# Triangular inverse from blocks of 4, decay formed in both orientations, decay rows loaded a head ahead, a semaphore per merged block, and a plain last store, in a one-core hybrid decoder layer

## The chip, the cores and the metric

One Trainium2 chip, one of its cores. The metric is the device time of one execution in microseconds. TensorE is called PE, VectorE DVE, ScalarE ACT, GpSimd POOL and SyncE SP, as in the profile's rows.

## The reference

One decoder layer on x of 512 tokens by 2048 channels, float32. h is the RMS-normed x. One projection of h gives the q, k, v, z of eight delta-rule heads (branch A, 128 wide), beta and alpha of each, the q, k, v, z of eight block-sparse attention heads (branch B), and two gates of 2048 channels. Branch A is what the change is about:

```python
cum_g = jnp.cumsum(g, axis=-1)
decay_mat = jnp.exp(jnp.where(causal, cum_g[..., :, None] - cum_g[..., None, :], -jnp.inf))
kk = jnp.einsum("nbhid,nbhjd->nbhij", k, k)
a_mat = jnp.where(strict, beta[..., :, None] * kk * decay_mat, 0.0)
sol = lax.linalg.triangular_solve(eye + a_mat, rhs, left_side=True, lower=True, unit_diagonal=True)
...
merged = jax.nn.sigmoid(g_gdn) * y_gdn + jax.nn.sigmoid(g_moba) * y_moba
x = x + jnp.einsum("btd,de->bte", merged, w_o[l])
```

The kernel uses chunks of 128 tokens in place of 64, four to a head, and forms the inverse of I + A instead of solving. Both branches then go through an up-projection to 2048 channels, are gated, added, and projected by w_o; x is added.

## The kernel before, in words

**Exact products.** Every large product of float32 matrices is three PE products of rounded parts: high by high, high by low, low by high. ACT makes the high part (`split` in the scalar block), DVE the low one.

**Head loop (0 to 977 us).** For each of eight heads, eight stripes of 128 columns of w_in are projected: `win(w, a, b)` issues the k-steps a to b of stripe w, 16 in all, each of three matmuls of 512 columns (lines 740 to 744). Between these pieces PE executes the small fp32 steps of the head: transposes and products of 128 x 128, one for each of four chunks (`four`, `turn`). The order on every engine is written out by hand in its `head(h, p)`; p is the head before, whose attention is finished in the first two stripes of the next head. Heads 1 to 6 are a hardware loop on DVE, ACT and POOL, heads 1 to 7 on PE; head 0 and the last one are written apart.

**The inverse.** L is minus the strict lower part of beta k k' decay. `cgrow` makes decayT = exp(row - column + mask); POOL masks it (`dTs`); DVE multiplies it with k k' (`kk`, into Up), PE transposes Up (`UT`), DVE multiplies the result by -beta (Ln), PE transposes that again (`LT`), and DVE cuts blocks of 16 out of both. `n1` to `n4` form (I + L)(I + L^2)(I + L^4)(I + L^8) for the blocks of 16. `ma` and `mb`, three times, merge two blocks each: to 32, to 64, to 128. `ma` multiplies the part of L below the diagonal blocks (`lm[1]`, `lm[2]`, masked by POOL) by the inverse so far and transposes the inverse; ACT and DVE copy the two results (Yt, XTt); `mb` multiplies them; DVE adds. The last merge works on corners of 64 x 64.

**Decay rows.** `cg_dram` holds the cumulated decay of each head as a row; POOL loads it, copied to all partitions, at the head's start (`decay_row`).

**Last head.** Ten steps `own_step` (2048 columns each, on DVE) put sums of parts of h into `own`, and POOL stores four stages of it (`store_own`); a step that overwrites the tile waits for the store before it.

**Products by quads (978 to 1642 us).** Gates (4 quads), up-projections (2 for each branch) and w_o (2 quads) are computed as 2 x 2 blocks with seven products instead of eight (P11, P12, PS1, PS2, PS4, PS3, P22). A unit is 1024 columns of weights; ACT rounds them (`op_hi`), DVE takes the rest (`op_lo`), four units ahead of PE. DVE's `block_add` finishes a block. In the quads YB and YB + 1 (branch B) DVE multiplies the block by its gate, and POOL adds branch A's block by an accumulating DMA (`finish_block`), one after the other, under the one semaphore `part_added`; PE then transposes the merged block (`merged_turn`). The quads from W0 on are stored by accumulating DMAs into `out`, where x has been copied before.

## Time and profile before

| | us |
|---|---|
| median of 3 runs (1638.84 to 1641.06) | 1639.57 |
| the profiled execution, its time | 1643.32 |
| its span, first to last instruction | 1641.8 |
| PE busy | 1592.5 (97%) |
| DVE busy | 1092.7 (67%) |
| ACT busy | 790.1 (48%) |
| POOL busy | 158.3 (10%) |
| mean granted PE clock | 0.994 |

A row of a timeline gives start and duration, engine, line and operation, output <- inputs, and in brackets how long the engine was idle before it and what released it. PE's rows overlap: a matmul's duration has its way through the array in it, so the cost of a group is read from the starts of what follows. PEld are weight loads. A plain fp32 matmul shows as two records (x8 is four matmuls), a transpose as one. DVE's durations overlap by some 0.08 us as well.

### The profile page before, as it was taken

The numbers are of one execution on the slowest core, as the hardware profiler recorded it, in microseconds if no ns is written. First come the engines' busy times: TensorE is split into PE (matmuls) and PEld (weight loads), VectorE is DVE, ScalarE is ACT, GpSimd is POOL, SyncE is SP. The second block draws the span as 40 slices with busy tenths as digits, with TensorE's granted clock in tenths as the row PEclk, the third lists the DMA queues.
The fourth block names the chain that finished last, engine by engine and source line by source line (L and its number), as shares of the span: only waits on it lengthen the run. The fifth ranks groups of instructions, "written<-read, shape, count | busy, mean of one in ns | idle before, by whom it ended". The sixth has DMA issues, their size and how long they took to land.

```text
span 1641.8 us, 20823 instructions
## 1 busy us (share of the span) xinstructions
PE 1592.5 (97%) x7858; PEld 1316.3 (80%) x7858; DVE 1092.7 (67%) x1320; ACT 790.1 (48%) x1048; POOL 158.3 (10%) x154
## 2 busy tenths in 40 slices
PE   6999999999999999999999999999999999999997
PEld 5888888887887887887887887888888778777885
DVE  5745745645646646556568758867677999888863
ACT  5434534435434444335335346556465845447442
POOL 4101001001001000010011011011010000001011
PEclk9999999999999999999999999999999999999999
DMA  8304314223223233133143337576566556775653
GB/s 261 78 26 115 84 38 129 57 76 90 77 57 99 73 77 96 51 89 83 51 113 101 137 136 210 192 192 220 140 189 187 196 196 209 202 217 112 196 116 52
DMA packets 192379, 206.19 MB, mean 126 GB/s; under 512 B 7491, under 2 KB 139846, under 8 KB 190726
## 3 DMA queue, kind: packets, MB, share of 16 engines
q1 hardware_dynamic: 176470, 161.69, 33.2%
q0 software_dynamic: 15856, 43.80, 11.2%
q8 instruction: 33, 0.54, 0.1%
q14 instruction: 20, 0.16, 0.0%
HBM read 180.28 MB, written 29.38 MB: 128 GB/s over the span
## 4 chain that ended last, share of the span: by engine, by line
PE 81%; issue 6%; DVE 5%; DMA 5%; ACT 2%; POOL 1%; SPq 0%; ACTq 0%; POOLq 0%; DVEq 0%
PE bank L740 14%; PE bank L744 14%; PE bank L742 14%; PE bank L1161 8%; PE bank L1163 8%; PE bank L1165 8%; PE bank L769 6%; DMA e_block<-branch_a 2%; PE bank L774 1%; DVE ring_lo L2117 1%; PE bank L930 1%; PE bank L946 1%; DMA operands<-branch_a 1%; ACT ring_hi L1520 1%; PE bank L940 1%
## 5 line engine op out<-in xcount | busy, mean ns | idle before, releaser
L740 PE MATMUL bank<-h_hi_r,w_hi 128*128 128x512 f32 x1008 | 421.5, 418 | 0.0
L744 PE MATMUL bank<-h_hi_r,w_raw_r 128*128 128x512 f32 x1008 | 396.9, 394 | 0.0
L742 PE MATMUL bank<-h_lo_r,w_hi 128*128 128x512 f32 x1008 | 394.1, 391 | 0.0
L2117 DVE TENSOR_TENSOR ring_lo<-operands,ring_hi 128x1024 fp32r<-128x1024 f32 x224 | 271.8, 1221 | 117.8 <-ACT ring_hi L1520 116.8
L1520 ACT ACTIVATE ring_hi<-operands 128x1024 fp32r<-128x1024 f32 x224 | 235.5, 1059 | 230.0 <-PE bank L1165 174.4
L744 PEld LDWEIGHTS bank<-h_hi_r,w_raw_r 128*128 128x128 f32 x1008 | 189.1, 188 | 43.0
L742 PEld LDWEIGHTS bank<-h_lo_r,w_hi 128*128 128x128 f32 x1008 | 190.3, 189 | 35.6 <-issue 1.7
L740 PEld LDWEIGHTS bank<-h_hi_r,w_hi 128*128 128x128 f32 x1008 | 189.9, 188 | 35.8 <-issue 1.7
L1161 PE MATMUL bank<-ring_hi,h_hi_r 128*128 128x512 f32 x480 | 190.6, 397 | 3.1 <-issue 3.1
L1163 PE MATMUL bank<-ring_lo,h_hi_r 128*128 128x512 f32 x480 | 189.4, 395 | 0.0
L1674 DVE TENSOR_TENSOR w_raw_r<-w_raw,w_hi 128x2048 fp32r<-128x2048 f32 x64 | 146.7, 2292 | 45.9 <-ACT w_hi L1219 44.7
L1165 PE MATMUL bank<-ring_hi,h_lo_r 128*128 128x512 f32 x416 | 162.4, 390 | 0.0
L1165 PE MATMUL bank<-ring_hi,sums_r 128*128 128x512 f32 x384 | 150.1, 391 | 0.0
L1161 PE MATMUL bank<-ring_hi,sums_r 128*128 128x512 f32 x320 | 126.3, 395 | 7.6 <-DVE ring_lo L2117 4.3
L1163 PE MATMUL bank<-ring_lo,sums_r 128*128 128x512 f32 x320 | 125.1, 391 | 0.0
L1219 ACT ACTIVATE w_hi<-w_raw 128x2048 fp32r<-128x2048 f32 x64 | 122.2, 1909 | 0.0
L1161 PEld LDWEIGHTS bank<-ring_hi,h_hi_r 128*128 128x128 f32 x480 | 90.4, 188 | 24.5 <-issue 4.1
L1163 PEld LDWEIGHTS bank<-ring_lo,h_hi_r 128*128 128x128 f32 x480 | 90.7, 189 | 18.5 <-issue 0.2
L1165 PEld LDWEIGHTS bank<-ring_hi,h_lo_r 128*128 128x128 f32 x416 | 78.4, 188 | 17.3
L1165 PEld LDWEIGHTS bank<-ring_hi,sums_r 128*128 128x128 f32 x384 | 72.5, 189 | 15.6
L1161 PEld LDWEIGHTS bank<-ring_hi,sums_r 128*128 128x128 f32 x320 | 60.4, 189 | 22.5 <-issue 7.2
L1163 PEld LDWEIGHTS bank<-ring_lo,sums_r 128*128 128x128 f32 x320 | 60.5, 189 | 12.3
(324 smaller groups left out, 2179.4 us busy)
## 6 DMA issues: line engine op xcount, KB each, us to landing
w_raw<-in_w_in_dram SPq DMA_DIRECT2D x64, 1024.0 KB, 6.0
operands<-in_w_in_dram SPq DMA_DIRECT2D x64, 512.0 KB, 4.7
operands<-in_w_o_dram SPq DMA_DIRECT2D x32, 512.0 KB, 4.9
operands<-in_w_in_dram POOLq DMA_DIRECT2D x16, 512.0 KB, 8.7
gates<-e_block POOLq DMA_DIRECT2D x16, 512.0 KB, 5.3
operands<-in_w_out_gdn_dram SPq DMA_DIRECT2D x16, 512.0 KB, 4.0
operands<-gates SPq DMA_DIRECT2D x16, 512.0 KB, 5.2
operands<-in_w_out_moba_dram SPq DMA_DIRECT2D x16, 512.0 KB, 4.6
```

The lines of the kernel that those rows point to most:

```text
L740: pe.matmul(PJ[slot % 2][:], w_hi[slot % 2][:, c], h_hi[:, k, :], start=(k == 0), stop=False, skip_group_check=True)
L742: pe.matmul(PJ[slot % 2][:], w_hi[slot % 2][:, c], h_lo[:, k, :], start=False, stop=False, skip_group_check=True)
L744: mm = pe.matmul(PJ[slot % 2][:], w_lo[slot][:, c], h_hi[:, k, :], start=False, stop=(k == KT - 1), skip_group_check=True)
L769: mm = pe.matmul(ps[:, tile4(t)], lhsT[:, tile4(t)], rhs[:, tile4(t)], start=True, stop=True)
L774: mm = pe.transpose(ps[:, tile4(t)], src[:, tile4(t)], ident[:])
L1161: pe.matmul(ps[:], a_hi, ring_hi[:, n % RINGS, c], start=(FRESH[p] and k == 0), stop=False, skip_group_check=True)
L1163: pe.matmul(ps[:], a_hi, ring_lo[:, n % RINGS, c], start=False, stop=False, skip_group_check=True)
L1165: mm = pe.matmul(ps[:], a_lo, ring_hi[:, n % RINGS, c], start=False, stop=(k == kn - 1), skip_group_check=True)
L1219: act.activation(w_hi[slot % 2][:], raw[slot][:], ACT.Copy).then_inc(s["hi_ready"], 1)
L1520: act.activation(ring_hi[:, n % RINGS, :], operand(q, p, j), ACT.Copy).then_inc(s["op_hi"], 1)
L1674: dve.tensor_tensor(w_lo[slot][:], raw[slot][:], w_hi[slot % 2][:].bitcast(F32), ALU.subtract)\
L2117: dve.tensor_tensor(ring_lo[:, n % RINGS, :], operand(q, p, j), ring_hi[:, n % RINGS, :].bitcast(F32), ALU.subtract).then_inc(s["op_lo"], 1)
```

## The change

- The inverse starts from blocks of 4: (I + L)(I + L^2), two small products instead of four steps, then five merges (to 8, 16, 32, 64, 128; `LEVELS`). A merge at level b of the first four moves only the 64 columns that belong to the lower halves of its pairs, and uses only the first 128 - b rows and columns; DVE masks the product while it copies it (`paired`), so L need not be masked ahead; ACT copies the transpose.
- The decay is formed in both orientations: `cgrow` makes dT and dL; POOL multiplies dL by -beta and by the mask of the blocks of 4, dT by that mask and by a row of -beta. DVE multiplies k k' by dTb and dLm (Ud, Ld), and by dL (Ln). The two transposes UT and LT are gone. `cg_dram` and `rows2` hold two rows a head, loaded while the head before runs. Head 0 gets its second row by four more matmuls, and one more transpose. `cgrow` stands ahead of `split(n + 1)` on DVE and ahead of `evac(p, 7)` on ACT.
- The masks are made at the start by nine DVE passes from the identity, which is loaded first.
- `own_step` 8 to 10 are cut into halves and stand at other places.
- `acc[i]`, one semaphore for each block, replaces `part_added`. For W0, POOL's `add_22` waits for the transpose of the block of the same number. In quads YB and YB + 1, `block_add` stands ahead of `op_lo`.
- The last block: x is loaded and added by DVE before PE is done, tile 0 is added when PE has finished it (`tile_done`), and SP stores both tiles plainly.

```diff
@@ sync @@
+            sp.dma_start(ident[:], consts[:, C_ID, :]).then_inc(s["ident_loaded"], 16)
             load_x(0)
             sp.dma_start(nw[:], norm_w.broadcast_to([P, D])).then_inc(s["nw_loaded"], 16)
-            sp.dma_start(ident[:], consts[:, C_ID, :]).then_inc(s["ident_loaded"], 16)
...
+            sp.dma_start(residual, token_block(xs, LAST, 3)).then_inc(s["stage_b"], 16)
+            for t in range(2):
+                sp.wait_ge(s["c_add"], 2 * (4 * LAST + 3) + 1 + t)
...
+                sp.dma_start(token_block(outs, LAST, 3)[:, t, :], block(LAST, 3)[:, t, :]).then_inc(s["stage_b"], 16)
+            sp.wait_ge(s["stage_b"], 16 * 5)
@@ gpsimd @@
+            def decay_parts(h):
+
+                pool.wait_ge(s["cg_dl"], h + 1)
+                pool.tensor_tensor(q4(dL), q4(dL), hcb(HC_NB), ALU.mult).then_inc(s["cg_dts"], 1)
...
+                pool.tensor_tensor(q4(dTb), q4(dT), over(masked4[:]), ALU.mult).then_inc(s["cg_dts"], 1)
...
+                pool.tensor_tensor(q4(dLm), q4(dL), over(masked4[:]), ALU.mult).then_inc(s["cg_dts"], 1)
...
+                pool.tensor_tensor(dTb[:], dTb[:], nb_row, ALU.mult).then_inc(s["cg_dts"], 1)
...
-                pool.wait_ge(s["cg_dt"], h + 1)
-                pool.wait_ge(s["n3_mm"], h)
-                pool.tensor_tensor(q4(dTs), q4(dT), over(plane(C_STRICT)), ALU.mult).then_inc(s["cg_dts"], 1)
+                decay_parts(h)
+                if p is None:
+                    store_rows()
+                if h is not last:
+                    decay_row(h + 1)
...
-                    if b > 0:
-                        pool.wait_ge(s["part_added"], 16 * b)
-                    pool.dma_start(e, m_dram[q - YB, k], accum_op=ALU.add).then_inc(s["part_added"], 16)
+                    pool.dma_start(e, m_dram[q - YB, k], accum_op=ALU.add).then_inc(acc[i], 16)
@@ tensor @@
             def n1(h):
...
-                four(G0, Ud, Ld)
-                four(G1, Ld, Ud).then_inc(s["n1_mm"], 1)
+                four(G0, Ud, Ld).then_inc(s["n1_mm"], 1)
...
             def ma(h, k):
...
+                    m = P - b
+                    for t in range(NT):
+                        pe.matmul(G0[:m, t * PAIRED:(t + 1) * PAIRED], Ln[:, t * P:t * P + m],
+                                  half_tile(xa, t, b, 1), start=True, stop=True)
+                    for t in range(NT):
+                        mm = pe.transpose(G1[:m, t * P:t * P + m], xa[:m, t * P:t * P + m], ident[:m, :m])
...
             def mb(h, k):
...
+                    m = P - LEVELS[k]
+                    for t in range(NT):
+                        mm = pe.matmul(G2[:m, t * PAIRED:(t + 1) * PAIRED], XTt[:m, t * P:t * P + m],
+                                       Yt[:m, t * PAIRED:(t + 1) * PAIRED], start=True, stop=True)
...
-                UT(h)
+                n1(h)
                 win(2, 12, 14)
                 ss(h, 1)
-                win(2, 14, 15)
-                LT(h)
-                win(2, 15, 16)
-                win(3, 0, 1)
+                win(2, 14, 16)
+                n2(h)
+                win(3, 0, 2)
                 qk(h)
...
+                win(4, 10, 12)
                 vTs(h)
...
+                win(4, 12, 13)
+                pe.wait_ge(s["X"], NL * h + NL - 1)
+                pe.wait_ge(s["vb"], h + 1)
                 win(4, 13, 14)
-                ma(h, 2)
+                ma(h, 4)
@@ vector @@
             def kk(h):
                 dve.wait_ge(s["kk_mm"], h + 1)
-                dve.wait_ge(s["cg_dts"], h + 1)
...
-                dve.tensor_tensor(Up[:], G2[:], dTs[:], ALU.mult).then_inc(s["kkd"], 1)
+                dve.wait_ge(s["cg_dts"], 4 * h + 4)
...
+                dve.tensor_tensor(Ud[:], G2[:], dTb[:], ALU.mult).then_inc(s["Ud"], 1)
...
+                dve.tensor_tensor(Ld[:], G2[:], dLm[:], ALU.mult).then_inc(s["Ld"], 1)
...
+                    dve.tensor_tensor(y, g, pairs, ALU.mult).then_inc(s["Y"], 1)
...
+                    b, m = LEVELS[k], P - LEVELS[k]
+                    x = half_of(xa, b, 1)[:m]
+                    g = compact(G2, m).rearrange("p (n b) -> p n b", b=b)
+                dve.tensor_tensor(x, g, x, ALU.add).then_inc(s["X"], 1)
```

The order of the instructions, at three places. First PE in the head loop, from the first step behind `kk` to the transposes of v. The rows of projection between them are left out; `work` and `inv` are the tiles of the powers and of the inverse. Before:

```order
L774 MATMUL bank<-ident,lower 128x128 x4
...
L769 MATMUL bank<-work 128x128 x8
...
L769 MATMUL bank<-work 128x128 x8
L769 MATMUL bank<-inv_a,work 128x128 x4
...
L769 MATMUL bank<-inv_b,lower 128x128 x4
L774 MATMUL bank<-ident,inv_b 128x128 x4
```

Now:

```order
L818 MATMUL bank<-inv_a,work 128x128 x4
...
L894 MATMUL bank<-inv_a,lower 124x64 x4
L897 MATMUL bank<-ident,inv_a 124x124 x4
...
L912 MATMUL bank<-work 124x64 x4
...
L894 MATMUL bank<-inv_a,lower 120x64 x4
L897 MATMUL bank<-ident,inv_a 120x120 x4
```

The long groups of full products are gone; between the pieces of projection there are now smaller groups, two for each merge.

Second DVE in the loop, between `n2` and the merge of blocks of 8 (`pairs` is the mask). Now:

```order
L1813 TENSOR_TENSOR work<-bank,pairs 124x256
...
L1709 TENSOR_TENSOR w_raw_r<-w_raw,w_hi 128x2048
L1828 TENSOR_TENSOR inv_a<-bank,inv_a 124x64x4
...
L1813 TENSOR_TENSOR work<-bank,pairs 120x256
...
L1741 TENSOR_SCALAR conv_gv<-raw_gv,chan 128x512
```

The split of a weight stripe stands between Y(0) and X(0), and the convolution of v between Y(1) and X(1).

Third DVE at the end of the program, behind PE's last units. Before:

```order
L2130 TENSOR_TENSOR e_block<-e_block,bank 128x512 x2
L2117 TENSOR_TENSOR ring_lo<-operands,ring_hi 128x1024 x4
L2132 TENSOR_TENSOR e_block<-bank,e_block 128x512 x4
```

Now:

```order
L2187 TENSOR_TENSOR e_block<-e_block,bank 128x512 x2
L2167 TENSOR_TENSOR ring_lo<-operands,ring_hi 128x1024 x4
L2189 TENSOR_TENSOR e_block<-bank,e_block 128x512 x2
L2373 TENSOR_TENSOR e_block<-e_block,operands 128x1024
L2189 TENSOR_TENSOR e_block<-bank,e_block 128x512 x2
```

The pass that adds x stands between the third block and the last one.

## Rows read from the trace of the kernel before

**Rows 1.** Busy time by stretch: us, PE, PEld, DVE, ACT, POOL, clock, DMA share, GB/s

```profile
153.08:270.81 117.73, 117.73 (x616) 97.77 (x615) 65.97 (x99) 50.88 (x77) 9.37 (x8) 1.00 0.29 79
```

**Rows 2.** Timeline of PE in head 1, projection rows left out

```profile
188.15 0.60 PE L774 MATMUL bank<-ident,work 128*128 128x128 f32 x4
...
213.27 1.05 PE L769 MATMUL bank<-inv_b,lower 128*128 128x128 f32 x8
214.16 0.60 PE L774 MATMUL bank<-ident,inv_b 128*128 128x128 f32 x4
...
216.68 1.06 PE L769 MATMUL bank<-work 128*128 128x128 f32 x8
...
219.66 1.05 PE L769 MATMUL bank<-inv_a,lower 128*128 128x128 f32 x8
...
226.14 0.67 PE L863 MATMUL bank<-inv_b,lower 64*64 64x64 f32 x8
226.75 0.41 PE L866 MATMUL bank<-ident,inv_b 64*64 64x64 f32 x4
```

**Rows 3.** Timeline of PE's weight loads in head 0

```profile
51.32 0.30 PEld L1075 LDWEIGHTS bank<-mgt,ones_f 128*128 128x128 f32 x2
51.55 0.19 PEld L740 LDWEIGHTS bank<-h_hi_r,w_hi 128*128 128x128 f32 x1
```

**Rows 4.** Timeline of DVE in head 1, and its first pass of head 2

```profile
186.65 0.68 DVE L1738 TENSOR_TENSOR work<-bank,work 128x512 f32<-128x512 f32 x1
...
199.18 2.55 DVE L1709 SCALAR_TENSOR_TENSOR conv_gv<-raw_gv,chan,conv_gv 128x512 f32<-128x512 f32 x3
...
212.09 0.69 DVE L1784 TENSOR_TENSOR v_beta<-bank,hcol 128x512 f32<-128x512 f32 x1 [1.85 <-PE bank L774]
...
270.81 2.29 DVE L1674 TENSOR_TENSOR w_raw_r<-w_raw,w_hi 128x2048 fp32r<-128x2048 f32 x1 [6.20 <-ACT w_hi L1219]
```

**Rows 5.** Timelines of POOL and DVE in the last head

```profile
895.89 3.28 POOL L654 TENSOR_TENSOR lower<-lower,cst 128x512 f32<-128x512 f32 x1 [13.11 <-DVE lower L1743]
...
898.44 1.28 DVE L1727 TENSOR_TENSOR conv_gq<-conv_gq,raw_gq 128x512 f32<-128x512 f32 x1 [0.44 <-ACT raw_gq L1286]
```

**Rows 6.** Timelines of ACT, DVE, POOL and PE in head 0

```profile
60.79 0.63 ACT L1261 ACTIVATE decayT<-decayT 128x512 f32<-128x512 f32 x1
...
60.66 4.09 DVE L1709 SCALAR_TENSOR_TENSOR conv_gq<-raw_gq,chan,conv_gq 128x512 f32<-128x512 f32 x3
...
62.89 1.30 POOL L644 TENSOR_TENSOR work<-decayT,cst 128x512 f32<-128x512 f32 x1
...
65.86 0.66 PE L774 MATMUL bank<-ident,conv_gk 128*128 128x128 f32 x4 [0.25 <-DVE conv_gk L1727]
```

**Rows 7.** Timeline of POOL in the last head, and DMA issues: count, size, median us

```profile
916.67 0.53 POOL L673 DMA_DIRECT2D row_sums<-sg  x1 [15.29 <-DVE sg L2077]
...
row_sums<-sg POOLq DMA_DIRECT2D x4, 1024.0 KB, 6.1
```

**Rows 8.** PE's waits (total, times, longest), and PE and ACT behind the merged blocks

```profile
PE bank L1177 <- DMA e_block<-branch_a: 5.7, 5, 1.9
...
1484.58 0.76 PE L1161 MATMUL bank<-ring_hi,sums_r 128*128 128x512 f32 x1 [3.29 <-issue]
...
1478.16 1.92 ACT L1607 ACTIVATE sums_r<-h_hi 128x2048 fp32r<-128x2048 f32 x1 [3.67 <-DVE h_hi L2077]
```

**Rows 9.** PE alone by stretch, behind an idle time of 3.12 us: us, busy, clock, DMA

```profile
1340.00:1345.00 5.00, 5.00 (x16) 0.66 1.02 373
```

**Rows 10.** DVE and POOL at the end, and DMA issues: count, size, median us

```profile
1629.91 1.29 DVE L2132 TENSOR_TENSOR e_block<-bank,e_block 128x512 f32<-128x512 f32 x2 [7.47 <-PE bank L1165]
...
1631.50 1.20 POOL L714 DMA_DIRECT2D out_dram<-e_block  x1 [7.56 <-DVE e_block L2132]
...
out_dram<-e_block POOLq DMA_DIRECT2D x8, 512.0 KB, 7.1
branch_outputs<-work POOLq DMA_DIRECT2D x8, 256.0 KB, 2.3
```

More of the change, by code:

```diff
@@ L53 @@
 NQ = W0 + W_QUADS
+LAST = NQ - 1
 BLOCK_ROW, BLOCK_COL = (0, 0, 1, 1), (0, 1, 1, 0)
@@ L101, in added @@
 def added(q):
-    return 16 * (sum(ku(b) == 4 for b in range(q)) + 1)
+    return 16 * (sum(ku(b) == 4 or b >= YB for b in range(q)) + 1)
 def op_loads(q, j, slot, nth=0):
@@ L278, in hybrid_layer @@
         w0_ = sb("work0", [P, T], at=area)
-        lm = [sb(f"lower{i}", [P, T], at=area) for i in range(3)]
+        Ln, dL, dLm = [sb(f"lower{i}", [P, T], at=area) for i in range(3)]
         xa = sb("inv_a", [P, T], at=area)
@@ L782, in cgrow @@
                                    start=True, stop=True)
+                for t in range(NT):
+                    mm = pe.matmul(G1[:, tile4(t)], hcol[:, HC_NB, t:t + 1].broadcast_to([P, P]), ident[:],
+                                   start=True, stop=True)
                 mm.then_inc(s["cgrow_mm"], 1)
@@ L856, in ma @@
-                if k < 2:
-                    pe.wait_ge((s["L32m"], s["L64m"])[k], h + 1)
-                    four(G0, lm[k + 1], src)
-                    mm = turn(G1, src)
+                    pe.wait_ge(s["X2"], h + 1)
+                    pe.wait_ge(s["qkd"], h + 1)
+                elif k < NL - 1:
+                    pe.wait_ge(s["X"], NL * h + k)
+                if k == NL - 1:
+                    for t in range(NT):
+                        i, j = tile4h(t)
+                        pe.matmul(G0[:P // 2, j], Ln[P // 2:, i], xa[P // 2:, j], start=True, stop=True)
+                    for t in range(NT):
+                        i, j = tile4h(t)
+                        mm = pe.transpose(G1[:P // 2, i], xa[:P // 2, i], ident[:P // 2, :P // 2])
@@ L1687, in cgrow @@
                     dve.wait_ge(s["cg_rows"], 16 * (NT + h))
-                row = G2 if first else cgb
+                row = G2 if first else cg_row
                 dve.wait_ge(s["hcol"], h + 1)
-                dve.wait_ge(s["cg_dts"], h)
-                for t in range(NT):
-                    dve.scalar_tensor_tensor(dT[:, tile4(t)], row[:, tile4(t)], hcol[:, HC_CG, t:t + 1],
-                                             plane(C_DMASK), ALU.subtract, ALU.add).then_inc(s["cg_arg"], 1)
+                dve.tensor_tensor(q4(dL), q4(row), hcb(HC_CG), ALU.subtract).then_inc(s["cg_arg"], 1)
+                dve.wait_ge(s["cg_arg"], 3 * h + 1)
+                dve.tensor_tensor(q4(dT), q4(dL), over(plane(C_DMASK)), ALU.add).then_inc(s["cg_arg"], 1)
+                dve.tensor_tensor(q4(dL), q4(dL), over(plane(C_CMASK)), ALU.subtract).then_inc(s["cg_arg"], 1)
             def conv(h, c):
@@ L2124, in block_add @@
                 e, p = block(q, i), BLOCK_PRODUCT[i]
-                dve.wait_ge(s["pe_unit"], ended(q, p))
+                tiles_apart = q == LAST and i == 3
+                if not tiles_apart:
+                    dve.wait_ge(s["pe_unit"], ended(q, p))
                 dve.wait_ge(s["e_copy"], 8 * q + (2, 6, 8, 8)[i])
@@ L2288, in _ @@
                 q, p, j = place(n)
+                for qb in range(NQ):
+                    for i in range(4):
+                        if YB <= qb < W0 and n == ended(qb, BLOCK_PRODUCT[i]) + LEAD - 1:
+                            block_add(qb, i)
                 op_lo(n)
@@ L2291, in _ @@
                     for i in range(4):
-                        if n == ended(qb, BLOCK_PRODUCT[i]) + LEAD - 1:
+                        if not YB <= qb < W0 and n == ended(qb, BLOCK_PRODUCT[i]) + LEAD - 1:
                             block_add(qb, i)
```

405 lines of the change are left out of this document (207 added, 198 removed).

## The prediction, before the changed kernel was run

> **What bounds the kernel now.** I read the busy time by stretch first. One pass of the head loop takes 117.7 us and TensorE (PE) is busy for all of it [rows 1]; so in seven of the eight heads only what PE executes, or a wait that does not exist yet, can move the time. Then the PE timeline inside one head, for the price of each record [rows 2, 3]; then VectorE (DVE) and ScalarE beside it, for the room each hand-over has [rows 4]; last PE's waits outside the loop [rows 6 to 8] and what follows PE's last matmul [rows 10].
>
> **Prices on PE.** A plain fp32 matmul is two records, a transpose one, a projection matmul (512 columns) one. In [rows 2] the first inverse step runs 8 records from 213.27 to 214.16: 0.111 us each. From 213.27 to 216.68 stand 8 records, 4 transposes and 9 projection matmuls (3.41 us); from 216.68 to 219.66 8 records and 9 projection matmuls (2.98). So 4 transposes cost 0.43 (0.108 each) and a projection matmul 0.23. The 64-column corner takes 0.61 for 8 records, 0.076 each.
>
> **1. The inverse on PE.** Removed per head: 40 full matmuls (4 of the first squaring's 8, 8 of the 12 behind it, the 12 of n3 and n4, the 16 of the first two merges) and 16 transposes (UT, LT and two merges): 80 + 16 = 96 records, at 0.111 10.7 us. Added: 32 matmuls that move 64 columns (64 records) and 16 transposes, all with 124, 120, 112 or 96 weight columns. No row has 124 x 64. Below, the 64 x 64 price, 0.076. Above, 0.111: two weight loads whose matmuls move only 32 columns still stand 0.115 apart [rows 3], so fewer moving columns alone bring nothing; the load seems to set the pace. I take a price that falls with the weight columns, between 0.076 at 64 and 0.111 at 128: 0.109, 0.107, 0.102, 0.094, mean 0.103. 80 records: 8.2 us. **Saved: 2.4 us a head, 19.4 in eight** (14.2 if all cost 0.111; 33 if the 64 half-width records cost 0.076).
> The Trainium skill (TensorE: Matmul & The Clock Gate, section LDWEIGHTS) gives the load as weight columns / 1.2 ns, which is 94 ns as a mean of the four widths; by it, with the 0.004 by which the measured 0.111 stands above its 107 ns, the sum would be 2.8 us a head. The 0.115 rows agree with its value for 128 columns.
>
> **2. Room of each hand-over in a steady head.** Ten steps of the merge take turns with three k-steps of projection (9 matmuls, 2.1 us). Counting in my prices from n2 as zero: qk 2.3, ma0 5.2, mb0 8.6, ma1 11.5, mb1 14.9, ma2 17.9, mb2 21.3, ma3 24.2, mb3 27.6, transposes of v 29.9.
> - n1 now needs two products (Ud, Ld) at kk instead of one. The one of before starts at 186.65; two at a spacing of 0.60 end at 187.95, and the step in that slot starts on PE at 188.15 [rows 2, 4]: covered by 0.2 us.
> - The split of 2.3 us between Y(0) and X(0): 7.1 to 9.4, PE's mb0 ends 9.7. Covered.
> - The convolution of v, 3.6 us (three taps are 2.55 [rows 4], with the first tap and the clamp), lies between Y(1) and X(1): 13.4 to 17.1, X(1) at 17.5, ma2 due at 17.9. Covered by 0.4, the tightest.
> - SiLU of v: ScalarE's three passes end at 22.4, X(2) at 23.3, ma3 due at 24.2. Covered by 0.9.
> - ma4 now waits for vb in the same window: the transposes last 0.60 [rows 2], DVE 0.69 more [rows 4] with 0.04 between, so vb stands 1.33 after their start; PE arrives after 0.43 + 3 x 0.23 = 1.12. **New wait 0.2 us a head, 1.8 in all** (0 to 6: the 0.4 and 0.2 above may not hold).
> - The decay: three 512-wide DVE passes instead of four small ones, one more exponential, four POOL passes instead of three. DVE sits idle for 6.2 us at the head's start [rows 4] and rows are loaded a head ahead, so the passes fall in there; POOL's four end some 25 us before kk. Nothing in heads 1 to 7. Without that idle time DVE would owe 2 us.
>
> **3. Head 0 has no such room.** PE: 4 more matmuls for the second row (0.89) and one transpose: +1.0. Then POOL's four passes (1.3 each alone [rows 6]) start when the second exponential is done. The first ran from 60.79 [rows 6]; PE's row is 0.9 later and ScalarE has a copy and an exponential more, so POOL starts at some 62.7. There DVE is about to begin the taps of q, 2 us later than the 60.66 of before (0.9 from PE, 0.8 from its own three wider passes, 0.3 for a second copy). A POOL pass and a DVE pass with two SBUF inputs shut each other out: POOL's pass stretches from 1.30 to 3.28, DVE's norm from 0.69 to 1.28 [rows 4 to 6], and three taps took 4.09 beside one POOL pass and its DMAs, 2.55 without [rows 4, 6]. Alternating, the taps end near 67.9, POOL near 69, the norm of k at 69.6, and PE, ready at 66.6 (65.86 less its wait of 0.25 [rows 6], plus 1.0), waits 3.0 instead of 0.25. n1 then waits 1.3 where its slot waited some 0.3 (kk stands behind a split of 2.3). Together some +3.4. A wait of this length is the sort after which the clock fell: after 3.1 us idle, the next 5 us ran at a mean of 0.66 [rows 9], 1.7 us lost; I put in half, 0.8. **Head 0: +5.2** (1 to 9).
>
> **4. Last head.** own_step 8 moves to 3.6 us after own_step 7; before there were 9. It overwrites what a POOL DMA of 1 MB still reads, issued as soon as step 7 ends and landing after 6.1 (median) [rows 7]. DVE then waits 2.7 us, with split(n+5) and Y(3) queued behind it, and PE's mb3 has 1.3 of room less the 1.2 us half-step: **+2.5** (0 to 6).
>
> **5. Merged blocks.** PE waits 5.7 us in five places for the adding DMAs [rows 8], each of which waited for the one before. With a semaphore each they go out when the product is gated, and block_add no longer queues behind op_lo (1.1 us earlier); landing 7 us later is in time. I call 4.1 of it the first quad's (three waits of 0.9 to 1.9) and book that. The second quad's share I give back: behind it PE waits 3.29 at 1484.58 for the first row sum, whose rounding on ScalarE had waited 3.67 for DVE's step [rows 8]; DVE's queue, not the DMA, sets that, so the wait grows to 5. **-4.1** (2 to 6).
>
> **6. Last store.** Now DVE adds from 1629.91 to 1631.20 behind PE, then the adding DMA leaves at 1631.50 and the span ends at 1641.8 [rows 10]. New: tile 0 is added while PE works, tile 1 ends at 1630.6, and a plain 256 KB store leaves. Plain 256 KB stores land in 2.3 us, adding ones of 512 KB in 7.1 [rows 10]; between 2.3 and 5, with issue and the closing waits, I take the end at 1634.8: **-7** (5 to 8.5). Block 2's adding DMA, issued 8.7 us earlier than the last, would land about then too.
>
> Constants first (ident before x) and the nine mask passes of DVE: the second x tile, which the start waits for, is issued third or fourth as before; 0 (-0.3 to +0.6).
>
> **Sum:** -19.4 + 1.8 + 5.2 + 2.5 - 4.1 - 7 = -21.0 us. The profiled execution took 1643.3 (span 1641.8), the median of the runs is 1639.6; with the same difference: **1619 us**.
>
> **Rivals.**
> - **A, width counts, not weights:** half-width records at 0.076. 64 x 0.027 x 8 = 14 more: 1605. For it: the corner's 0.076; against: the 0.115 of [rows 3]. 0.13.
> - **B, the steps get tight:** X(1) or Ld comes late and each head pays about 1 us: 1627. For: 0.2 and 0.4 us of room; against: the engines' chains are fixed ones of known length and nothing else stands in those queues. 0.14.
> - **C, the end stays:** the third block's adding DMA or POOL's closing wait ends last, so the last store brings 2, not 7: 1624. 0.10.
> - **D, slower, pieces:** the merges read and write pieces of 4, 8, 16 or 32 words with gaps, where all is contiguous before. If a record that moves such pieces takes more than twice its 0.1 us, or a DVE pass over them more than its room, PE gains nothing. At 0.21 a record instead of 0.103, the 32 piecewise records a head cost 3.4 us more: +27, 1646. It decides from 0.19 a record on. No row shows pieces so short; against it, the corner's tiles (64 in 128) run at 0.076. 0.05.
> - The forecast keeps 0.58.
>
> **Range and chances.** Worst sum of likely ends (records at 0.111, head 0 +8, last head +5, tail -5) gives 1632; the best (half the way to A, head 0 +2, last head 0) 1606. The range **1606 to 1632** leaves out D and the far half of A. A measurement here can tell about 0.2%, 3.3 us, from no change: slower by that needs D, 0.05; within it, B and all bad ends together, 0.04; faster 0.91.
>
> **What would show it.** Steady heads: period 115.5 us (117.7 before), 113.8 if A holds; a wait of some 0.2 us before the 64-column corner and nothing else over 0.3. The 124 x 64 group of 12 records in 1.3 us. In head 0 a wait of about 3 us before the transposes of k with DVE's taps stretched beside POOL; in the last head one before mb3. At the merges no DMA wait in the first quad, but a longer one at the row-sum product behind the second. The end 5 us after PE's last matmul. Wrong it would be if the periods were not below 117, or if waits of 1 us stood in every head.

## The result, and the profile after

The changed kernel took **1625.3 us** (median of 4 runs, 1624.4 to 1626.5), the kernel before beside it 1640.3 (1638.8 to 1641.9): ratio 0.991, 95% interval [0.989, 0.992], 15.0 us less. The forecast was 1619 in a range of 1606 to 1632. The direction and the range held, but the sum of 21 us was made of terms of which only some were right, and their errors partly cancelled.

A steady head, by stretch, from the transposes of k in head 1 to those in head 2 (columns as in [rows 1]):

```profile
185.79:300.67 114.88, 114.71 (x599) 94.96 (x598) 65.26 (x99) 50.77 (x76) 12.16 (x9) 1.00 0.31 83
```

Before it was 117.73 [rows 1]: 2.85 us less. TensorE is still busy for all but 0.17 us. Its rows in head 3, projection rows left out, answer to [rows 2]:

```profile
428.37 0.98 PE L894 MATMUL bank<-inv_a,lower 128*124 128x64 f32 x8
429.18 0.59 PE L897 MATMUL bank<-ident,inv_a 124*124 124x124 f32 x4
...
434.62 0.95 PE L894 MATMUL bank<-inv_a,lower 128*120 128x64 f32 x8
435.41 0.58 PE L897 MATMUL bank<-ident,inv_a 120*120 120x120 f32 x4
...
440.79 0.91 PE L894 MATMUL bank<-inv_a,lower 128*112 128x64 f32 x8
441.53 0.55 PE L897 MATMUL bank<-ident,inv_a 112*112 112x112 f32 x4
...
446.86 0.81 PE L894 MATMUL bank<-inv_a,lower 128*96 128x64 f32 x8
447.51 0.50 PE L897 MATMUL bank<-ident,inv_a 96*96 96x96 f32 x4
```

Read from start to start, the eight records of ma take 0.81, 0.79, 0.74 and 0.65 us: 0.101, 0.099, 0.093 and 0.081 each as a mean over the group, where I had put 0.109 to 0.094 and a full record of before takes 0.111 [rows 2]. What a record costs inside the group stands under experiments 4 and 5.

Head 0, DVE's timeline (the taps of q, the clamp, the norm of k), answer to [rows 6]:

```profile
62.61 4.92 DVE L1744 SCALAR_TENSOR_TENSOR conv_gq<-raw_gq,chan,conv_gq 128x512 f32<-128x512 f32 x3
67.56 1.37 DVE L1747 TENSOR_SCALAR raw_gq<-conv_gq 128x512 f32<-128x512 f32 x1
68.85 0.68 DVE L1762 TENSOR_TENSOR conv_gk<-conv_gk,raw_gk 128x512 f32<-128x512 f32 x1
```

POOL's timeline beside it:

```profile
62.54 1.04 POOL L683 TENSOR_TENSOR lower<-lower,hcol 128x512 f32<-128x512 f32 x1 [22.07 <-ACT lower L1304]
63.54 1.75 POOL L687 TENSOR_TENSOR work<-decayT,masked 128x512 f32<-128x512 f32 x1
65.25 1.73 POOL L690 TENSOR_TENSOR lower<-lower,masked 128x512 f32<-128x512 f32 x1
66.94 1.71 POOL L694 TENSOR_TENSOR work<-work,decay_rows 128x512 f32<-128x512 f32 x1
```

PE's waits outside the steady heads, from its timeline (in brackets the wait and what ended it):

```profile
69.58 0.66 PE L823 MATMUL bank<-ident,conv_gk 128*128 128x128 f32 x4 [2.99 <-DVE conv_gk L1762]
74.23 1.13 PE L818 MATMUL bank<-work 128*128 128x128 f32 x8 [1.02 <-DVE work L1773]
...
853.34 0.46 PE L976 MATMUL bank<-ident,bv 128*128 128x128 f32 x1 [3.82 <-DVE bv L1913]
...
919.53 1.54 PE L912 MATMUL bank<-work 96*96 96x64 f32 x8 [4.14 <-DVE work L1813]
...
1474.60 0.77 PE L1198 MATMUL bank<-ring_hi,sums_r 128*128 128x512 f32 x1 [8.27 <-issue]
```

Head 0 waits as forecast (3.0 and 1.3). At 919.53 stands the wait of the last head that was forecast (2.5), at 853.34 one that was not. No transpose of a merged block waits 0.25 us or more for its DMA, and the row-sum product behind the second quad waits 8.27 instead of 3.29 [rows 8].

The first of the two on DVE's timeline of the last head (its last row belongs to the second wait):

```profile
837.49 2.35 DVE L2142 TENSOR_TENSOR sg<-h_hi_r 128x1024 f32<-128x1024 f32 x2
839.88 2.36 DVE L2142 TENSOR_TENSOR sg<-sg,h_lo_r 128x1024 f32<-128x1024 f32 x2
842.15 0.68 DVE L1725 TENSOR_TENSOR lower<-decay_rows,hcol 128x512 f32<-128x512 f32 x1
...
847.16 3.47 DVE L1709 TENSOR_TENSOR w_raw_r<-w_raw,w_hi 128x2048 fp32r<-128x2048 f32 x1 [2.99 <-ACT w_hi L1258]
...
915.71 1.23 DVE L2142 TENSOR_TENSOR sg<-h_hi_r 128x1024 f32<-128x1024 f32 x1 [4.38 <-DMA row_sums<-sg]
```

POOL beside it:

```profile
848.44 3.31 POOL L694 TENSOR_TENSOR work<-work,decay_rows 128x512 f32<-128x512 f32 x1
```

DVE at the same place of head 6:

```profile
722.72 0.69 DVE L1725 TENSOR_TENSOR lower<-decay_rows,hcol 128x512 f32<-128x512 f32 x1
...
728.85 2.37 DVE L1709 TENSOR_TENSOR w_raw_r<-w_raw,w_hi 128x2048 fp32r<-128x2048 f32 x1 [4.11 <-ACT w_hi L1258]
```

own_step 1 and 2 (4.7 us) stand ahead of the decay passes. These passes now stand ahead of the split of the next stripe, and their exponentials ahead of ScalarE's rounding that the split waits for. The passes are 4.5 us later than in head 6 (842.15 less 114.88 is 727.3), the split 3.4, and it stretches from 2.4 to 3.5 beside POOL's fourth pass. The clock behind the two waits (by stretch; PEclk is the third number from the end):

```profile
853.00:858.00 5.00, 4.66 (x13) 3.47 (x14) 3.75 (x9) 2.28 (x7) 0.00 (x0) 0.66 0.00 0
919.00:924.00 5.00, 4.47 (x17) 3.79 (x18) 3.49 (x6) 1.89 (x3) 0.00 (x0) 0.50 0.00 0
```

The tail, answer to [rows 10]: first DVE's two tiles, then SP's two plain stores. PE's last matmul starts at 1619.55.

```profile
1618.70 0.69 DVE L2189 TENSOR_TENSOR e_block<-bank,e_block 128x512 f32<-128x512 f32 x1 [5.06 <-PE bank L1202]
1619.97 0.69 DVE L2189 TENSOR_TENSOR e_block<-bank,e_block 128x512 f32<-128x512 f32 x1 [0.58 <-PE bank L1202]
```

The stores, from the DMA issues (count, size, median us to landing):

```profile
out_dram<-e_block SPq DMA_DIRECT2D x2, 256.0 KB, 2.2
```

The span ends at 1623.3, 3.8 us after PE's last start; before it was 12.3 (1629.5 to 1641.8).

**The ledger.** I take landmarks on PE: the transposes of k in head 0 (65.86 before, 69.58 now), the corner's mb of each head, the product of the second row sum, the last matmul.

| stretch | forecast | measured |
|---|---|---|
| eight heads, 2.82 a head with the new wait in it | -17.6 | -22.6 |
| head 0 beside that | +5.2 | +4.1 |
| last head beside that (corner to corner 127.2 now, 118.3 before) | +2.5 | +11.8 |
| merged blocks to the row sum | -4.1 | see below |
| end | -7 | -8.5 |

Without the fourth line that is -15.2, and the medians say -15.0. The two profiled spans say -18.5 (1641.8 to 1623.3). The difference is the fourth line. The profiled execution of before lay 3.0 us above its kernel's median (1643.3 against 1640.3), that of the changed kernel 0.45 below.

### The profile page after: what moved, and what is told of

It reads as the page before. It is cut to its first block, busy times and chain, and to the rows that moved or that the text cites. A ratio compares the mean times of both kernels' runs of the same rounds, so it can differ in the third digit from the quotient of the medians.

```text
span 1623.3 us, 20700 instructions
## 1 busy us (share of the span) xinstructions
PE 1572.4 (97%) x7739; PEld 1297.6 (80%) x7739; DVE 1091.4 (67%) x1333; ACT 788.8 (49%) x1049; POOL 176.4 (11%) x161
## 4 chain that ended last, share of the span: by engine, by line
PE 83%; DVE 10%; issue 3%; DMA 2%; ACT 2%; SPq 0%; POOL 0%; DVEq 0%; ACTq 0%
PE bank L789 14%; PE bank L793 13%; PE bank L791 13%; PE bank L1198 10%; PE bank L1200 10%; PE bank L1202 10%; DVE ring_lo L2167 2%; PE bank L818 2%; PE bank L912 1%; PE bank L894 1%; PE bank L966 1%; PE bank L982 1%; DVE w_raw_r L1709 1%; PE bank L897 1%; PE bank L823 1%
```

## Experiments

Each ran beside the kernel before, whose median in the four sessions was 1641.0, 1641.8, 1640.4 and 1640.8. "The changed kernel" is 1625.3 throughout, from a session of its own; since the same kernel moved by 1.5 us between sessions, a difference of that size from it shows nothing by itself.

### 1. The decay rows ahead of the own steps (e1_rows_first)

```diff
                     columns(h)
+                    cgrow(h)
                     if h is last:
                         own_step(1)
                         own_step(2)
-                    cgrow(h)
                     split(n + 1, 1)
```

> In the last head the changed kernel's PE waits 3.82 us at 853.34 for softmax's bv and runs at a granted 0.66 behind it (head period 120.6 instead of 114.9, so 5.7 us). Here own_step 1 and 2 stand behind cgrow instead of ahead of it, nothing else moves. Theory 'queue': the 4.7 us of own steps held back the decay rows, and with them ScalarE's two exponentials and the rounding that the split waits for; the split was due at 843.7 and own steps now end at some 844.2: wait under 0.5 us, about 5.5 us gained, 1620. Rival 'shared port': POOL's four decay passes (4.9 us alone) now run beside the four own halves, which read two SBUF tiles each; they shut each other out, own steps end at 848 to 849 instead of 844, the split starts there, and PE's wait is 4 to 6 us again: 1625 to 1627.

Measured 1627.1 (1626.0 to 1627.4), ratio 0.991 [0.990, 0.993]: no gain. DVE's timeline in the last head:

```profile
839.31 3.20 DVE L2142 TENSOR_TENSOR sg<-h_hi_r 128x1024 f32<-128x1024 f32 x2
842.54 4.44 DVE L2142 TENSOR_TENSOR sg<-sg,h_lo_r 128x1024 f32<-128x1024 f32 x2
846.91 3.38 DVE L1709 TENSOR_TENSOR w_raw_r<-w_raw,w_hi 128x2048 fp32r<-128x2048 f32 x1
```

POOL's:

```profile
841.39 2.27 POOL L687 TENSOR_TENSOR work<-decayT,masked 128x512 f32<-128x512 f32 x1
843.63 2.27 POOL L690 TENSOR_TENSOR lower<-lower,masked 128x512 f32<-128x512 f32 x1
845.86 2.28 POOL L694 TENSOR_TENSOR work<-work,decay_rows 128x512 f32<-128x512 f32 x1
```

The rows come at their place, but the four own halves take 7.6 us instead of 4.7 and POOL's passes 2.3 instead of 1.3. The split ends where it ended in the changed kernel (850.3 and 850.6), and PE waits 3.44. The theory "queue" fell and the rival "shared port" held: whichever of the two stands first, 4.7 us of own steps and 4.9 us of POOL passes do not fit ahead of the split. The Trainium skill (SBUF — State Buffer, section SBUF: two separate sides) calls the port pair of the two engines an exclusive lock held for a whole instruction. The trace comes close to that: a POOL pass follows the next after 2.24 us here, where one takes 1.27 alone and a DVE half pass 1.17, 2.44 together.

### 2. The own steps moved away from both places (e2_spread)

Step 1 stands where 3 stood, 2 where 4 stood, 3 where 5 stood; 4 and 5 behind mb0 and mb1, 6 behind mb3, 7 behind mb4. POOL's stores of them follow: the first stands with the second and third, the last behind its other stores. And:

```diff
                 kS(h, 3)
+                if h is last:
+                    own_step(8)
+                    own_step(9)
                 o_lo_(h)
...
                 bvTs(h)
+                if h is last:
+                    own_step(10)
```

> All ten own steps of the last head move later, into idle places of DVE behind the decay rows (1 in the slot of 3, 2 in that of 4, 3 in that of 5, 4 and 5 behind mb0 and mb1, 6 behind mb3, 7 behind mb4, 8 and 9 behind the last kS, 10 behind bvTs), and POOL's stores follow them. If both waits of the last head (3.82 at 853.34, 4.14 at 919.53, each with a clock of 0.5 to 0.66 behind it) are made by where the own steps stand, both vanish, the last head's period becomes 114.9 to 115.5 and the gain over the changed kernel is 11 to 12.5 us: 1613 to 1614. If the rows' new exponentials and POOL's four passes are what makes the last head late by themselves, the first wait stays (gain 6). If the sums come too late for the first sum product (998 in the changed kernel), a wait appears there instead, 1616 to 1620.

Measured **1614.0** (1613.4 to 1614.1), ratio 0.984 [0.982, 0.985]. Both waits are gone, and from head 6 to the last head it takes what a steady head takes (by stretch, from the transposes of k to those of the last head):

```profile
760.20:875.08 114.88, 114.71 (x599) 94.97 (x598) 70.24 (x103) 50.74 (x76) 11.60 (x8) 1.00 0.29 78
```

So the last head's 11.8 us are the placing of ten passes, of which the change moved only the last three, and the decay's new passes by themselves cost that head nothing.

### 3. Only the step that waited for its store, and those behind it (e10_own8)

```diff
-                if h is last:
-                    own_step(8, 0)
                 split(n + 5, 1)
                 ma(h, 3)
                 zclamp(h, 0)
-                if h is last:
-                    own_step(8, 1)
                 mb(h, 3)
+                if h is last:
+                    own_step(8, 0)
                 vTs(h)
+                if h is last:
+                    own_step(8, 1)
...
```

Steps 9 and 10 and POOL's last store move back with it, to the places that the expectation gives.

> The changed kernel with own_step 8 behind mb3 (halves around the transposes of v), 9 behind mb4 and split(n + 6), 10 behind the last kS, POOL's last store behind its others: own steps 1 to 7 stay. Theory: step 8 then starts some 10 us after the store of step 7 was issued, so DVE does not wait for it; PE's wait of 4.14 before mb3 and the slow clock behind it go, 5.5 to 6.1 us, and the first wait of 3.8 stays: 1619 to 1620. Rival 'the waits hide each other': the second wait moves to another place of the last head, 1623 to 1625.

Measured 1619.7 (1618.1 to 1621.0), ratio 0.987 [0.986, 0.989]. The wait at 919.53 is gone, that of 3.81 at 853.68 stays. So 5.7 us belong to the store that step 8 waited for, and the 5.7 that experiment 2 gained beyond it belong to the start of the head.

### 4 and 5. What sets the price of a small record (e3_w128, e4_mov128)

All 128 weight columns with 64 moved, and then the other way round:

```diff
-                        pe.matmul(G0[:m, t * PAIRED:(t + 1) * PAIRED], Ln[:, t * P:t * P + m],
+                        pe.matmul(G0[:, t * PAIRED:(t + 1) * PAIRED], Ln[:, t * P:(t + 1) * P],
                                   half_tile(xa, t, b, 1), start=True, stop=True)
```

> ma's first product loads all 128 weight columns in the four piecewise merges instead of 124, 120, 112 and 96; it still moves 64. Theory 'weights set the pace': its 8 records take 0.89 us instead of 0.81, 0.79, 0.74 and 0.65, 0.57 us a head more, steady period 115.45 instead of 114.9, total +4.5 us, 1630. Rival 'the rows moved or the output's rows set it, and 0.08 to 0.11 is only the spread of small matmuls': no change, 1625.3.

```diff
-                        pe.matmul(G0[:m, t * PAIRED:(t + 1) * PAIRED], Ln[:, t * P:t * P + m],
-                                  half_tile(xa, t, b, 1), start=True, stop=True)
+                        pe.matmul(G0[:m, t * P:(t + 1) * P], Ln[:, t * P:t * P + m],
+                                  xa[:, t * P:(t + 1) * P], start=True, stop=True)
```

> The same product with the weights of the change (124 to 96 columns) but all 128 columns of the inverse moved instead of 64; DVE reads the needed half out of the product in pieces. Theory 'weights set the pace': 8 records stay at 0.81, 0.79, 0.74, 0.65 or rise little, steady period within 0.1 us of 114.9, 1625 to 1626. Rival 'moving columns set the pace' (rival A of the prediction): up to 0.89 each, +0.5 us a head or more, 1630. DVE's piecewise read of the product costs at most some tenths beside PE; if it makes a wait, it shows before mb.

Measured 1627.9 (1625.2 to 1630.5) and 1628.6 (1626.8 to 1629.7), ratios 0.993 [0.991, 0.994] and 0.992 [0.991, 0.994]. The steady period tells it better, 115.30 and 115.45 against 114.9 (of the sum over eight heads, the last head's first wait swallows a part: 2.6 instead of 3.8 in both). PE's timeline at the last piecewise merge, of the first kernel:

```profile
448.07 1.00 PE L894 MATMUL bank<-inv_a,lower 128*128 128x64 f32 x8
448.91 0.50 PE L897 MATMUL bank<-ident,inv_a 96*96 96x96 f32 x4
```

Of the second:

```profile
448.65 1.03 PE L894 MATMUL bank<-inv_a,lower 128*96 128x128 f32 x8
449.52 0.49 PE L897 MATMUL bank<-ident,inv_a 96*96 96x96 f32 x4
```

| eight records of ma, start to start | weight columns 124, 120, 112, 96 |
|---|---|
| full weights, 128 moved (before, [rows 2]) | 0.89 for 128 |
| full weights, 64 moved | 0.84, 0.84, 0.83, 0.84 |
| narrow weights, 128 moved | 0.87, 0.87, 0.88, 0.87 |
| narrow weights, 64 moved (the change) | 0.81, 0.79, 0.74, 0.65 |

These are sums over a group. Read record by record, the first spacing in a group differs from the others, and they tell more:

| from one record's start to the next | first | the others |
|---|---|---|
| full weights, 128 moved (before) | 0.108 | 0.112 |
| full weights, 64 moved | 0.055 | 0.112 |
| narrow weights, 128 moved | 0.109 | 0.109 at all four widths |
| narrow weights, 64 moved (the change) | 0.055 | 0.108, 0.105, 0.098, 0.085 |
| the corner, 64 weight columns, 64 moved | 0.106 | 0.058, and 0.149 behind the last |

My theory held for the first kernel and fell for the second: with 128 columns moved, weights of 96 columns bring nothing. Loads and matmuls overlap, and the spacings are those of the longer of two times: one that follows the weight columns (0.112 at 128 down to 0.058 at 64), and one that follows the moved ones (0.109 at 128, 0.055 at 64). The narrow load pays because the half-width move is short enough to let it. Both narrowings are needed, and rival A was right that the width counts.

The Trainium skill (TensorE: Matmul & The Clock Gate, section LDWEIGHTS) has the load at weight columns / 1.2 ns: 107, 103, 100, 93 and 80 ns from 128 to 96, and 53 for the corner's 64. The trace agrees: the spacings are 5 ns above it at all six widths. The sum made by that page, 2.8 us a head, came nearer than mine of 2.4. The other bound, 0.109 us for 128 moved columns, is the figure of these runs.

### 6. The last store of before (e5_store_old)

```diff
-            dve.wait_ge(s["stage_b"], 16 * 3)
-            dve.wait_ge(s["e_copy"], 8 * LAST + 8)
-            e = block(LAST, 3)
-            dve.tensor_tensor(e[:], e[:], residual, ALU.add).then_inc(s["a_step"], 1)
             block_add(LAST, 3)
...
+            finish_block(NQ - 1, 3)
```

SP's loads and stores of this block are left out as well.

> The changed kernel with the last store of before: both tiles added at once when PE is done, then one adding DMA of 512 KB by POOL, no x tile loaded ahead. Theory: the new end alone is worth the whole shortening of the tail, 12.3 us from PE's last matmul to the end of the span before and 3.8 after, so 8.5: 1633 to 1634, and the tail is 12.3 again. Rival C of the prediction (something else ends last, the store brings 2): 1627.

Measured 1634.7 (1633.1 to 1636.5), ratio 0.996 [0.994, 0.997], 9.4 us above the changed kernel; from PE's last start to the end it took 12.5. The whole shortening of the tail counts, and rival C is out.

### 7 and 8. Merged blocks: the chain, and the place of block_add (e6_chain, e9_badd_old)

```diff
                     pool.wait_ge(e_stored[k], stored(q - 2))
+                    if b > 0:
+                        pool.wait_ge(acc[(i + 3) % 4], added(q if i else q - 1))
                     pool.dma_start(e, m_dram[q - YB, k], accum_op=ALU.add).then_inc(acc[i], 16)
```

> The changed kernel with each adding DMA of branch A waiting for the one before, as before; block_add's new place stays. Theory: the waits of before at the transposes of the merged blocks come back (5.7 us in five places, less 1.1 us at each by block_add's earlier place), and the wait at the row-sum product behind the second quad shrinks by what the second quad's waits take, so 1 to 3 us net: 1627 to 1628. Rival 'block_add's place did it': no wait comes back, 1625. Rival 'the whole 5.7 was given up': 1631.

Measured 1625.7 (1624.4 to 1628.3), ratio 0.991 [0.989, 0.992]: no difference. Two of the waits come back, and the one at the row-sum product is shorter by 2.0 (PE's timeline):

```profile
1414.53 1.09 PE L1218 MATMUL bank<-ident,e_block 128*128 128x128 f32 x8 [0.48 <-DMA e_block<-branch_a]
...
1464.66 1.09 PE L1218 MATMUL bank<-ident,e_block 128*128 128x128 f32 x8 [1.58 <-DMA e_block<-branch_a]
...
1474.81 0.77 PE L1200 MATMUL bank<-ring_hi,sums_r 128*128 128x512 f32 x1 [6.26 <-issue]
```

Then block_add behind op_lo again, the semaphores kept:

```diff
-                        if YB <= qb < W0 and n == ended(qb, BLOCK_PRODUCT[i]) + LEAD - 1:
-                            block_add(qb, i)
                 op_lo(n)
...
-                        if not YB <= qb < W0 and n == ended(qb, BLOCK_PRODUCT[i]) + LEAD - 1:
+                        if n == ended(qb, BLOCK_PRODUCT[i]) + LEAD - 1:
                             block_add(qb, i)
```

> The changed kernel with block_add behind op_lo again in the two quads of branch B; the semaphore for each block stays. Theory 'two covers for one wait': each adding DMA leaves 1.1 us later, and of the changed kernel's slack at the transposes (0.5 to 1.5 us where the chained run still had no wait) nearly all is used up: waits under 0.5 us return in one or two places, 1625.3 to 1626.5; chain and place together took out the 4 us, neither alone. Rival 'the place did it' (the chained run lost only 0.6 us): waits of 1 us in four or five places, 1628 to 1629.

Measured 1624.3 (1624.0 to 1627.5), ratio 0.991 [0.989, 0.993]: again no difference, waits of 0.60 and 0.38 come back, and the one at the row sum is 5.32. Neither part has a worth of its own that these runs can show. Both taken back at once was not run.

The new place of block_add also brings a wait that I had not seen. DVE now comes to the multiplication by the gate before that gate has been loaded, and the whole queue to the row sum stands behind it. In the changed kernel (DVE's timeline; the second row is the sum's low part, which ends 0.11 us before PE's product starts):

```profile
1451.97 1.23 DVE L2198 TENSOR_TENSOR e_block<-e_block,operands 128x1024 f32<-128x1024 f32 x1 [1.43 <-DMA operands<-gates]
...
1472.21 2.28 DVE L2203 TENSOR_TENSOR sums_r<-h_hi,sums_r 128x2048 fp32r<-128x2048 f32 x1
```

All eleven profiles with block_add in its new place have such a wait here, of 1.2 to 2.7 us. With block_add in its old place, in e9_badd_old and in both profiles of before, there is none. From the last head's corner to the row-sum product e9_badd_old took 543.5 us, the changed kernel 545.1. How much of the time it is worth was not measured: the medians differ by 1.0 us.

### 9. The kernel before once more (e12_before_again)

> The kernel before once more, unchanged, for a second profile. Between the two profiled executions the change was worth 18.5 us, between the medians 15. Theory: the first profiled execution lay 2 to 3 us above its kernel's own middle, by slower stretches of PE outside the head loop; a second one then has the same head period (117.7), the same waits before the second row-sum product (sum of all waits within 1 us), the same tail of 12.3 and a span of 1638 to 1641. Rival: the difference is in a part that the change removed, so that its size there is not a constant: the waits at the merged blocks or the tail differ by over 1 us.

Median 1641.5 of 10 runs, ratio 1.0006 [0.9996, 1.0015]; the profiled span is 1637.2, 4.6 below the first. Head period, last head (118.25 from corner to corner) and tail (12.4) are those of the first. The waits at the merged blocks are not (PE's waits, total, times, longest; [rows 8] had 5.7 in five):

```profile
PE bank L1177 <- DMA e_block<-branch_a: 3.9, 3, 2.0
```

The rival holds: that wait is no constant. The three waits of the first quad, from which I had booked 4.1, are a single one of 1.67 here, and another of 3.12 further ahead (at 1339.73, the one of [rows 9]) is 1.30. From the corner's mb of the last head to the row-sum product it is 548.3 us in the first profile of before and 544.4 in this one, mean 546.3. In the changed kernel and the seven others that leave this part as it has it (experiments 1 to 6 and the late POOL passes below) it is 545.1 to 548.5, mean 546.2. Two profiles of before that lie 4 us apart cannot fix such a term to 1 us, but the medians leave no room for it in the ledger either (-15.0, and -15.2 without it). These runs show no gain of 4.1, nor any at all.

### 10 and 11. Who sets the wait behind the second quad (e7_step20, e11_sumfirst)

On top of experiment 2, the second half of the row sum right behind the first:

```diff
-            merged_at = {unit(W0 - 1, PS3, 0): (P11, None), unit(W0, P11, 3): (None, 19), unit(W0, PS1, 1): (None, 20),
+            merged_at = {unit(W0 - 1, PS3, 0): (P11, None), unit(W0, P11, 3): (None, (19, 20)),
```

> e2_spread, and in the first units of w_o the second half of the row sum (step 20 on DVE) stands right behind the first half instead of behind two op_lo and one form_t1 (3.4 us). Theory 'DVE's queue sets the wait behind the second merged quad': ScalarE's rounding of the sum starts 3.4 us earlier, PE's wait falls from 8.6 to about 5.5, 3 us gained: 1611. Rival 'the copy of the transposed block or ScalarE sets it': no change, 1614.

Measured 1611.0 (1610.8 to 1612.8), ratio 0.982 [0.980, 0.983], 3.0 below experiment 2. PE's wait is 5.56 instead of 8.62, as reckoned from DVE's queue alone (PE's timeline):

```profile
1459.50 0.76 PE L1198 MATMUL bank<-ring_hi,sums_r 128*128 128x512 f32 x1 [5.56 <-DVE sums_r L2201]
```

Then, in its place, both halves ahead of that unit's form_t1, and the sum's low part two units earlier:

```diff
+                if n == unit(W0, P11, 3):
+                    merged_step(19)
+                    merged_step(20)
                 forms(q, n)
...
-            merged_at = {unit(W0 - 1, PS3, 0): (P11, None), unit(W0, P11, 3): (None, 19), unit(W0, PS1, 1): (None, 20),
-                         unit(W0, PS1, 2): (PS1, 21), unit(W0, PS1, 3): (None, 22), unit(W0, PS2, 1): (PS2, None),
+            merged_at = {unit(W0 - 1, PS3, 0): (P11, None), unit(W0, PS1, 0): (PS1, None),
+                         unit(W0, PS1, 2): (None, 21), unit(W0, PS1, 3): (None, 22), unit(W0, PS2, 1): (PS2, None),
```

> e2_spread, with steps 19 and 20 of the first row sum ahead of the form_t1 of their unit, and the sum's low part on DVE two units earlier (behind the op_lo of the first PS1 unit). Theory 'one DVE queue': against e7_step20 the sum is formed 1.1 us earlier and its low part no longer queues behind two op_lo (2.3 us), so PE's wait falls from 5.56 to 2 to 2.5 us: 1607.5 to 1608.5. If the next units' low parts come late instead, waits of 1 to 2 us stand at the products after it: 1609 to 1610.

Measured **1609.4** (1608.6 to 1610.2), ratio 0.981 [0.980, 0.983], the fastest kernel of the study. The wait falls to 2.98 at 1456.90, but 2.12 appear at 1471.07 in front of the next row sum, so 1.5 are gained where 2.5 to 3.5 were expected, as the second case of the expectation has it (PE's timeline):

```profile
1456.90 0.47 PE L1198 MATMUL bank<-ring_hi,sums_r 128*128 128x512 f32 x1 [2.98 <-issue]
...
1471.07 0.47 PE L1198 MATMUL bank<-ring_hi,sums_r 128*128 128x512 f32 x1 [2.12 <-issue]
```

### 12. POOL's passes of head 0 held back (e8_pool_late)

```diff
                 pool.wait_ge(s["cg_dl"], h + 1)
+                if isinstance(h, int) and h == 0:
+                    pool.wait_ge(s["norm"], 1)
```

> The changed kernel, but in head 0 POOL's four decay passes wait until DVE has normed k. Theory 'port': the three taps of q take 2.4 us instead of 4.9 and the clamp 0.4 instead of 1.4, the norm of k stands at 66.0 instead of 68.9, and PE's wait there falls from 2.99 to under 0.4 us; the four passes then run beside the split and end at 73 to 75, so kk waits for them and gives 1 to 3 us back: 1623 to 1626. Rival 'DVE is late by its own passes': taps still above 4 us, wait still 3 us.

Measured 1627.5 (1624.9 to 1628.4), ratio 0.991 [0.990, 0.993]. DVE's timeline in head 0:

```profile
62.47 2.33 DVE L1746 SCALAR_TENSOR_TENSOR conv_gq<-raw_gq,chan,conv_gq 128x512 f32<-128x512 f32 x3
64.83 0.43 DVE L1749 TENSOR_SCALAR raw_gq<-conv_gq 128x512 f32<-128x512 f32 x1
65.17 0.68 DVE L1764 TENSOR_TENSOR conv_gk<-conv_gk,raw_gk 128x512 f32<-128x512 f32 x1
```

PE's:

```profile
66.30 0.60 PE L825 MATMUL bank<-ident,conv_gk 128*128 128x128 f32 x4
...
74.57 1.96 PE L820 MATMUL bank<-work 128*128 128x128 f32 x8 [4.69 <-DVE work L1775]
```

Without POOL beside them the taps take 2.33 and the clamp 0.43, and PE's wait for the norm of k is gone: the 2.6 and 0.9 us more came from POOL's passes beside them and from nothing else. But DVE's product kk now waits for those passes, PE waits 4.69 for it, and the clock falls behind that wait (0.66 over the next 5 us). Head 0 ends 1.9 us later than in the changed kernel. The cost of head 0 is moved by this, not removed.

## Why the prediction was right and wrong

- **Part 1, the inverse on PE: mechanism right, price too high.** The mean of the four widths is 0.093 us, not 0.103, and a head gained 2.8 and not 2.4 less 0.2. The step that failed is "a price that falls with the weight columns, between 0.076 at 64 and 0.111 at 128". The corner's 0.076 is a mean over a group that holds a long spacing at either end (0.106 and 0.149); inside it a record takes 0.058. A line from 0.058 at 64 to 0.112 at 128 gives 0.109, 0.105, 0.098 and 0.085, which is what experiments 4 and 5 show inside the groups. The half-width move makes the first spacing of each group short as well.
- **Part 2, room in a steady head: right.** No wait above 0.2 us. PE waits for the product of v in seven heads, 1.2 us in all (forecast 0.2 each). Rival B is out.
- **Part 2, the decay "nothing in heads 1 to 7": wrong in the last one.** I counted DVE's 6.2 us of idle time in head 1 [rows 4] as the cover and did not look whether the last head has it. There own_step 1 and 2 fill it. 5.7 us, of which 3.8 are wait and the rest clock (experiments 1 to 3).
- **Part 3, head 0: right.** k's transposes at 69.58, forecast 69.6; POOL from 62.54, forecast 62.7; the waits 2.99 and 1.02, forecast 3.0 and 1.3. The 0.8 for the clock was not there in this profile, where it stayed at 1.00. But it is a matter of the execution: in the profiles of experiments 3, 10 and 11, whose head 0 is the same and waits the same 2.98 to 2.99, the granted clock fell (0.66 to 0.68 over 68.5 to 73.5), n1's wait of 1.0 was gone for it, and the corner's mb of head 0 came 0.3 to 0.4 us later behind k's transposes.
- **Part 4, the last head's step 8: mechanism right, size half.** PE's wait was 4.14 where I had 2.5, since the store took 7.9 us (907.84 to 915.71) where I had put the median of 6.1, and the clock behind it, which I had left out here, cost some 1.5 to 2.5 more (5.7 in all by the medians of experiment 3, 6.6 by the landmarks of the ledger).
- **Part 5, merged blocks: wrong.** The failed step is "I call 4.1 of it the first quad's and book that". I gave back only the second quad's share, and let the wait at the row sum grow from 3.29 to 5. It grew to 8.27. The product starts when DVE's queue has got there, 16 us without a gap up to the sum's last step (1451.97 to 1468.15) and the low part behind it, so it takes back what PE gained ahead of it, from either quad. That run without a gap even begins with a wait of 1.43 for a gate (experiment 8). Experiments 10 and 11, which only shorten that queue, gained 3.0 and another 1.5. The one pair of profiles seemed to confirm a gain (-3.2); the second profile of before took that away.
- **Part 6, the last store: right, at the upper end** (8.5 where I had 7, given 5 to 8.5; the end 3.8 us after PE's last start instead of 5).
- **Rivals.** A in part (both widths count, but a half-width record does not cost 0.076, and the period is 114.9 and not 113.8), B and C out, D out: the piecewise records run at the price of contiguous ones or below. That the time lay in the range was luck as much as care: the heads gained 5 us more than I had and the end 1.5, the last head cost 9 more, and 4 at the merges were not there.

## What to carry to other kernels

A head, or any pass, that is written apart from the loop needs its own reading: the idle time that covers an added pass in the steady one may be filled there, and both large surprises here sat in the one head of eight that carries extra work. When a wait is removed upstream of a queue that runs without a gap, find the next place where PE meets that queue before booking anything. A price taken as the mean of a group of records holds the group's two ends; read the spacing inside it, and the line through the prices comes out straight. And a term read off one pair of profiles should be held against the difference of the medians: here 18.5 against 15.0 pointed to the term that was not there.

## What was not expected of the hardware

- A small fp32 record costs the longer of its load and its move, inside a group: 0.112 us with 128 weight columns, whether 64 or 128 are moved; 0.109 for 96 to 124 with 128 moved; 0.085 for 96 and 0.058 for 64 with 64 moved.
- The length of a wait did not decide alone whether the granted clock fell. One of 2.99 us in head 0 left it at 1.00 in the changed kernel, and one of 2.98 at the same place was followed by 5 us at 0.68 in experiment 3. The last head's first wait of 2.6 left it at 1.00 in experiment 4 and was followed by 5 us at 0.69 in experiment 5. Waits of 3.82, 4.14 and 4.69 were followed by 5 us at 0.66, 0.50 and 0.66. In the last head that cost some 1.5 to 2.5 us each beside the wait itself.
- A pass with a single tensor input was also held up beside POOL: the clamp took 1.37 us instead of 0.43.
- The wait for the same adding DMAs was 5.7 us in one execution of the kernel before and 3.9 in another, in the first quad alone 4.1 and 1.7.
